# One plain pair of up products of feed-forward 1 as a Strassen pair, its block differences moved from GpSimd to VectorE

## The reference

```python
hn = rmsnorm(x, ffn_norm_g[l])
gu = hn @ w_up[l]                                   # 1024x1024 by 1024x5632
h = jax.nn.silu(gu[..., :FFN_HIDDEN]) * gu[..., FFN_HIDDEN:]    # FFN_HIDDEN = 2816 = 22 x 128
x = x + h @ w_down[l]
```

## Time and profile before

| | |
|---|---|
| median of 3 runs | 3460.7 us (3460.41 to 3461.76) |
| profiled execution, its own time | 3463.52 us |
| its span, from the first to the last instruction | 3461.8 us |
| TensorE busy | 3363.3 us (97%) |
| VectorE / ScalarE / GpSimd busy | 1980.2 / 1330.5 / 440.9 us |
| first plain product of feed-forward 1 starts | 1384.5 us |
| Strassen pairs of feed-forward 1 | 1429.8 to 1811.3 us |

### The profile page before, as it was taken

One profiled execution on the slowest core, in us unless ns is written; L12 is line 12 of the kernel. 1 busy time (PEld: TensorE's weight loads), 2 busy tenths in 40 slices (PEclk: granted clock), 3 DMA queues, 4 the chain that ended last, 5 costly groups with the idle time before them and its releaser, 6 DMA issues.

```text
span 3461.8 us, 39444 instructions
## 1 busy us (share of the span) xinstructions
PE 3363.3 (97%) x16072; PEld 2743.1 (79%) x16072; DVE 1980.2 (57%) x2420; ACT 1330.5 (38%) x1876; POOL 440.9 (13%) x321
## 2 busy tenths in 40 slices
PE   8999999999999899999999999999899999999998
PEld 6888888877877688888888877787698778888886
DVE  8454462333745434677772374444675778888326
ACT  4232112444155523433331156344445454444213
POOL 0000000000000000444430010000000015544000
PEclk9999999999999999999999999999999999999999
DMA  3313341113400024232347322221203322333831
GB/s 121 75 52 114 106 164 63 50 50 96 163 30 28 25 75 134 82 120 104 116 156 294 104 79 101 67 92 47 82 1 128 122 86 110 110 110 136 319 104 49
DMA packets 114965, 351.71 MB, mean 102 GB/s; under 512 B 16072, under 2 KB 26056, under 8 KB 114768
## 3 DMA queue, kind: packets, MB, share of 16 engines
q1 hardware_dynamic: 112672, 348.86, 28.6%
q10 hardware_dynamic: 2112, 0.33, 0.1%
HBM read 265.01 MB, written 82.95 MB: 101 GB/s over the span
## 4 chain that ended last, share of the span: by engine, by line
PE 85%; DVE 7%; ACT 6%; issue 1%; DMA 1%; SPq 0%; ACTq 0%; DVEq 0%
PE PS L498 44%; PE PS L2466 21%; PE PS L481 8%; PE PS L3873 1%; PE PS L3885 1%; PE PS L1930 1%; PE PS L1952 1%; PE PS L1622 1%; PE PS L516 1%; PE PS L996 1%; ACT dS L1678 1%; DVE wlo L443 0%; ACT whi L438 0%; PE PS L3878 0%; PE PS L1597 0%
## 5 line engine op out<-in xcount | busy, mean ns | idle before, releaser
L443 DVE TENSOR_TENSOR wlo<-raw,whi 128x1024 fp32r<-128x1024 f32 (+3 forms) x380 | 481.9, 1268 | 400.8 <-ACT whi L438 398.1
L438 ACT CAST whi<-raw 128x1024 fp32r<-128x1024 f32 (+3 forms) x380 | 359.2, 945 | 694.7 <-PE PS L498 342.8
L498 PE MATMUL PS<-xhi,whi 128*128 128x512 f32 x1872 | 603.2, 403 | 12.7 <-DVE sbVt L2148 6.3
L498 PE MATMUL PS<-xlo,whi 128*128 128x512 f32 x1872 | 580.2, 391 | 0.0
L498 PE MATMUL PS<-xhi,wlo 128*128 128x512 f32 x1872 | 578.3, 390 | 0.0
L498 PEld LDWEIGHTS PS<-xhi,whi 128*128 128x128 f32 x1872 | 345.8, 189 | 99.0 <-issue 14.0
L498 PEld LDWEIGHTS PS<-xlo,whi 128*128 128x128 f32 x1872 | 353.3, 189 | 75.9
L498 PEld LDWEIGHTS PS<-xhi,wlo 128*128 128x128 f32 x1872 | 352.3, 188 | 75.4
L2466 PE MATMUL PS<-tf,whi 128*128 128x512 f32 x936 | 288.2, 389 | 0.0
L2466 PE MATMUL PS<-xhi,whi 128*128 128x512 f32 x624 | 243.3, 390 | 2.5 <-DVE xlo L2451 2.5
L2466 PE MATMUL PS<-xhi,wlo 128*128 128x512 f32 x624 | 243.5, 390 | 0.0
(11 more groups left out here) (589 smaller groups left out, 5643.9 us busy)
## 6 DMA issues: line engine op xcount, KB each, us to landing
raw<-in_w_up SPq DMA_DIRECT2D x88, 512.0 KB, 3.3
hid<-hs SPq DMA_DIRECT2D x88, 512.0 KB, 3.6
raw<-in_w_in SPq DMA_DIRECT2D x67, 512.0 KB, 3.3
slot<-hid SPq DMA_DIRECT2D x56, 512.0 KB, 6.8
adr<-in_w_ada SPq DMA_DIRECT2D x48, 512.0 KB, 4.6
raw<-in_w_down SPq DMA_DIRECT2D x40, 512.0 KB, 3.6
raw<-in_w_gate SPq DMA_DIRECT2D x32, 512.0 KB, 3.3
merged<-hid SPq DMA_DIRECT2D x16, 512.0 KB, 13.1
```

Source lines behind the costliest of these rows:

```text
L438: act.e.copy(whis[place(i)][:, ks, :], raws[i % RING][:, ks, :]).then_inc(*give("w_hi", i))
L443: dve.e.tensor_tensor(wlos[place(i)][:, ks, :], raws[i % RING][:, ks, :], whis[place(i)][:, ks, :].bitcast(F32), ALU.subtract).then_inc(*g ...
L498: ins = pe.e.matmul(ps[:, h * 512:(h + 1) * 512], w[s][:, k, :], x[:, h * 512:(h + 1) * 512], start=(at == 0 and n == 0), stop=(at == kt - ...
```

## The change

Pair 1 of feed-forward 1 becomes a Strassen pair (`PLAIN` goes from (2, 3) to (1, 3)). The input's block differences of feed-forward 1 move from GpSimd's queue to VectorE's, behind the gate of pair 0 and in front of the split of the next weights. The list `fast` is set anew in front of each run of Strassen pairs: banks 6 and 7, and then the banks of `dense` from the pair used longest ago. The semaphore `t_sum1` goes with its engine.

```diff
-PLAIN = (2, 3)
+PLAIN = (1, 3)
...
-    "sums_dve": "x_add sq_add t1_sum sum1 t2_sum t_sum2",
+    "sums_dve": "x_add sq_add t1_sum sum1 t2_sum t_sum1 t_sum2",
...
-    "sums_pool": "w_sum t_sum1 sv_w sv_c22 t1_add",
+    "sums_pool": "w_sum sv_w sv_c22 t1_add",
...
         def as_banks():
+            fast[:] = [6, 7] + [2 * p + x for p in dense for x in range(2)]
             for p in range(3):
                 bank.read_by[2 * p] = bank.read_by[2 * p + 1] = psum.read_by.get(p, ())
...
         def ffn_pool(pool, f):
-            if f == 1:
-                input_sums(pool, 1)
             plain = PLAIN[f - 1]
...
                 dve.e.tensor_tensor(FSG[i % 2], psum.of(j), rstd1, ALU.mult).then_inc(*give("f1_gate", i))
+                if i == 0:
+                    input_sums(dve, 1)
                 j = begin_dve(dve, "w_up", 22 + i)
```

## The result

The changed kernel takes 3465.34 us in the median of 21 runs, the kernel before 3460.41 us in 21 runs beside them: ratio 1.0014, 95% interval 1.0008 to 1.0020. It is slower, by 0.14%, some 4.9 us. The forecast was 3465.3 us and "within 0.2%".

A forecast was written before the change was run, and what follows sets the result against it. TensorE, busy 97% of the span, was taken to bound the kernel: -2.72 (matmuls) + 4.50 (wait) + 2.8 (clock) = +4.6 us on the median of 3460.7, giving 3465.3 us, range 3462.3 to 3467.9.

The forecast's parts named there:

- Matmuls, -2.72 us: TensorE in feed-forward 1: 12 matmuls fewer (96 - 84) at 0.227 us each, a gain of 2.72 us.
- The wait at p4, 4.50 us: First Strassen pair of feed-forward 1: TensorE asks at 1413.42, VectorE's low part of sum 4 arrives at 1417.92.
- The clock, 2.8 us: Behind the wait at p4: matmuls run at half clock for a while, losing 2.8 us, bounds 0 and 3.3.
- the third row: Feed-forward 2's 2.54 us wait: clock low 3.3 us after it, nine matmuls read as 0.37 us each, 1.65 us lost.
- +1.8 without a penalty: Whole kernel: the predicted change in time if the low clock cost nothing, +1.8 us instead of +4.6.
- rival 2: At p4 and p5: the wait comes but the clock stays up, p5 waits 0.6 us; +2.4, 3463.1 us; chance 0.10.
- The second wait, hidden at the low clock: At p5, for sum 1: 0.6 us of waiting at full clock, hidden because slow p4 lasts until about 1423.
- GpSimd out of the way: Beside VectorE's differences: GpSimd's weight sums for pair 1 done by about 1397, none of its work in 1400 to 1418.
- Banks: nothing gained: New bank order costs and gains nothing; the wait on the last result at the first down product, 0.70 us before, stays.
- No wait at p4: Rival at p4: the matmul gain arrives whole, needing 4.5 us less VectorE work; 3458.0 us; chance 0.06.
- The clock low for 13 us: Rival behind the wait at p4: 13.2 us at half rate lose 6.6; +8.4, 3469.1 us; chance 0.06.
- GpSimd beside the differences: Rival: GpSimd's weight sums hold VectorE up to 5.2 us more, wait 9.7; +10, 3470.7 us; chance 0.04.

The follow-up runs named there:

- the run with the differences short: Changed kernel with feed-forward 1's four block differences cut to 8 positions of each block, computation not whole; 3457.65 us against 3459.36 for the kernel before (0.9995).
- the one with more work: Changed kernel with the low part of sum 2 computed a second time on VectorE before the value of pair 0; 3469.11 us, 1.0030 against the kernel before.
- GpSimd's differences: Changed kernel with the block differences left in GpSimd's queue, one plain pair and new bank order kept; 3464.03 us, 1.0014 against the kernel before.
- the run with the differences early: Changed kernel with differences before the wait for the norm's root, ScalarE's high parts before the first silu, VectorE's low parts behind pair 0's gate; 3458.42 us, 0.9995.
- sum 4 in front: Changed kernel with sum 4's low part before the value of pair 0 and sum 2's behind it; 3467.81 us, 1.0025 against the kernel before.
- banks: Changed kernel with `fast` starting at the oldest dense pair, then banks 6 and 7, then the rest; 3461.76 us, 1.0007 against the kernel before.

## Why the prediction was right

**Matmuls, -2.72 us.** Right: 2.73 with nothing else in the way.

**The wait at p4, 4.50 us.** Right, 4.47 and 4.46 as the trace counts it. Each step of the queue came out as worked out, 0.8 us earlier as a whole because the gate of pair 0 started 0.8 us earlier in this execution: differences 8.93 us (8.93), the half split 0.60, two low parts 4.41 (4.40), value 1.13 (1.14), last low part 2.28 (2.27). That VectorE's queue sets it is shown from both sides, by the run with the differences short and by the one with more work. The prediction took the moment at which TensorE asks from the end of the matmul before, but the 2.72 us of the first term from starts; by starts throughout the wait is 4.62, so its sum was 0.1 us short in this term.

**The clock, 2.8 us.** The mechanism is right, the size too large: 2.15 us in the first trace, 1.7 to 3.1 in the others with a wait of 2.9 to 6.8 us. This is the one term that was clearly mis-sized; the sum +4.6 met +4.09 in the trace. The low stretch is as long as expected (6.8 us), but only 4.4 us of it lie behind the wait, where the prediction took the 5.5 and 6.2 us of its two rows. Its reading of the third row was also off: nine matmuls in 3.3 us count those that the edges of the stretch cut, and their spacing in the kernel before is not 0.37 us but 0.43, so that a slow matmul loses 0.20 of its 0.43 us, a little under half:

```profile
2845.67 0.63 PE L2466 MATMUL PS<-xhi,wlo 128*128 128x512 f32 x1
2846.10 0.63 PE L2466 MATMUL PS<-xhi,whi 128*128 128x512 f32 x1
2846.53 0.63 PE L2466 MATMUL PS<-xlo,whi 128*128 128x512 f32 x1
```

And its "+1.8 without a penalty" forgets the second wait of 0.6 us, which its rival 2 has: +2.4. That the median came out at 3465.34 against a forecast of 3465.3 is luck. The 4.9 us by which it moved has an interval of 2.8 to 6.9 us and is no evidence for the larger size; the second time it moved by 7.7.

**The second wait, hidden at the low clock.** Right: p5 follows p4 without a break; the low part of sum 1 is done at 1418.13 + 2.28 = 1420.41, and p5 starts at 1421.99.

**GpSimd out of the way.** Right: its weight sums for pair 1 are done by 1395.04 and the next begins at 1422.85.

```profile
1393.77 1.27 POOL L2437 TENSOR_TENSOR raw<-raw,raw 128x512 f32<-128x512 f32 x1
1422.85 1.29 POOL L2428 TENSOR_TENSOR raw<-raw 128x512 f32<-128x512 f32 x1 [27.80 <-DVE wlo L443]
```

What happens when this doesn't hold is shown by the runs with GpSimd's differences and with the early ones.

**Banks: nothing gained.** Right: L2527 is waited for 0.78 us after as before, and another list takes it away. That the old list could not simply be left alone is argued from the code and was not tried: without the new line, feed-forward 2 would begin its pairs with bank 1, whose last reader on ScalarE stands behind the copy of p1, which waits for TensorE; each would wait for the other. If that holds, one plain pair can't stand without the reset.

**The rivals.** No wait at p4: out, but it is what the short differences show to be possible. Clock stays up: out here; behind waits of 1.13 and 1.26 us it does stay up. The clock low for 13 us: out, 6.8 us at most in feed-forward 1. But the prediction's "none is longer" than 6.9 us holds for the waits of the kernel before only. At the wait of 4.88 us, in code that no run changed, the run with the differences early has 10.2 us of low clock:

```profile
2465.30:2475.50 10.20, 5.96 (x27) 5.59 (x28) 7.29 (x18) 0.97 (x3) 0.00 (x0) 0.50 0.55 196
```

So the upper side had more to it than the chance of 0.06 was worked out from. GpSimd beside the differences: out in the changed kernel, and real, at 2.2 us, in my early variant.

## What to carry to other kernels

A step that is taken out of the bounding engine is also cover for what is prepared behind it: here 2.7 us of matmuls went and 21.8 us of lead with them, and the price was where the lead ran out. Add up the helper engine's queue from a known start to the new deadline, with durations of the same instruction elsewhere in the trace; there may be a second deadline just behind the first. Then look for the idle stretch in that queue before the work, and check what shares it.

## What the hardware showed unexpectedly

What a wait costs besides its own length did not grow with it. It went by where the low clock fell: sometimes within the wait, sometimes only after work had resumed.

| run | wait, us | clock low from, to | work resumes | lost besides, us |
|---|---|---|---|---|
| kernel before, feed-forward 2 | 2.54 | 2845.7, 2849.1 | 2844.41 | 1.7 |
| differences on GpSimd | 2.90 | 1414.5, 1421.3 | 1415.40 | 3.1 |
| sum 4 in front | 3.65 | 1424.3, 1427.7 | 1423.20 | 1.8 |
| banks | 4.46 | 1415.8, 1419.2 | 1414.94 | 1.7 |
| changed kernel | 4.47 | 1414.7, 1421.5 | 1417.12 | 2.2 |
| more work | 6.79 | 1419.4, 1426.2 | 1421.60 | 2.3 |

The shortest wait in feed-forward 1 with a low clock behind it lost the most, and one and the same wait of 4.46 us lost 1.7 or 2.2. Each loss is the extra time of the two block products behind the wait.

Code that nobody touched moves by more than the change: the norm's sum of feed-forward 1 starts at 1394.41 and 1396.71 us in two executions of the changed kernel, and between 1390.99 and 1397.16 over all kernels here, while the length behind it repeats to 0.03 us. For an effect of a tenth of a percent inside one stretch, the trace of the stretch told in one run what eleven runs of the whole did not. It can't speak for the rest of the kernel, though: three of the medians here moved by 3 to 4 us more than their stretch.
